# The next head pair's query and key work moved ahead of the present pair's output and retention end, on three engines

## What is computed

```python
def hybrid_layer(x, ...):
    proj = (_rms(x) * norm1_g) @ w_in
    aq, ak, av, rw, rq, rk, rv, rg, gates = _split(proj, IN_SIZES)
    aq = _rms(aq.reshape(B, T, ATTN_Q_HEADS, HEAD_DIM)) * attn_q_norm_g   # 8 heads of 64
    ak = _rms(ak.reshape(B, T, ATTN_KV_HEADS, HEAD_DIM)) * attn_k_norm_g
    o_a = sliding_window_attention(aq, ak, av, attn_sinks) @ w_attn_o
    o_b = rwkv7_time_mix(...) @ w_rwkv_o
    o_c = retention(rq, rk, rv, rg) @ w_ret_o
    ...

def retention(q, k, v, gate):
    qh, kh = _rotary(q, pos), _rotary(k, pos) * (d ** -0.5)
    s = jnp.einsum('bnihd,bnjhd->bnhij', qc, kc) * dmat
    inner = jnp.einsum('bnhij,bnjhe->bnihe', s, vc)
    kv = jnp.einsum('bnjhd,bnjhe,hj->nbhde', kc, vc, zeta)
    _, r_prev = lax.scan(step, 0, kv)            # R * chunk_decay + kv
    cross = jnp.einsum('bnihd,nbhde,hi->bnihe', qc, r_prev, xi)
    return _rms(inner + cross) * silu(gate)
```

## Time and profile before

| | |
|---|---|
| median of 3 runs | 3236.26 us (3235.94 to 3243.79) |
| the profiled execution | 3238.96 us |
| its span on the core | 3237.1 us |
| PE busy | 3112.4 us (96%) |
| DVE, ACT, POOL busy | 1140.9, 1100.4, 1432.6 us |
| mean granted clock of TensorE | 0.986 |

### The profile page before, as it was taken

The page is one execution under the profiler, slowest core; times in us unless marked ns, Lnnn a source line. Parts: engine busy times, 40 slices in busy tenths (PEclk is TensorE's granted clock), DMA queues, the critical chain, the costliest instruction groups (busy, mean ns, idle before and its releaser), DMA issues.

```text
span 3237.1 us, 52473 instructions
## 1 busy us (share of the span) xinstructions
PE 3112.4 (96%) x20754; PEld 2479.8 (77%) x20754; DVE 1140.9 (35%) x1645; ACT 1100.4 (34%) x1547; POOL 1432.6 (44%) x1824
## 2 busy tenths in 40 slices
PE   9999889999999999999989999999999998999999
PEld 6887678868878767887667888787788766788877
DVE  3026532361101446322555322226523255542210
ACT  4455543342222433113443322223311344432222
POOL 3532244635555444223325655565421242565555
PEclk9999999999999999999999999999999999999999
DMA  5233332213223232115214222233211331422223
GB/s 219 94 104 118 118 104 85 98 52 104 96 98 104 73 109 98 61 61 192 74 67 149 94 97 97 98 110 111 98 64 61 144 118 53 159 96 92 97 98 123
DMA packets 102130, 330.89 MB, mean 102 GB/s; under 512 B 10064, under 2 KB 10448, under 8 KB 101200
## 3 DMA queue, kind: packets, MB, share of 16 engines
q1 hardware_dynamic: 75088, 272.87, 24.7%
q10 hardware_dynamic: 26880, 55.65, 4.8%
HBM read 299.64 MB, written 28.84 MB: 101 GB/s over the span
## 4 chain that ended last, share of the span: by engine, by line
issue 41%; POOL 30%; PE 24%; DVE 2%; DMA 1%; ACT 1%; DVEq 0%; POOLq 0%; SPq 0%; ACTq 0%
POOL w_lo L317 30%; PE psum L346 19%; PE psum L682 4%; DMA H<-scratch 1%; DVEq L1507 0%; DMA arena<-in_w_ada 0%; POOLq L313 0%; PE psum L878 0%; PE psum L896 0%; PE psum L858 0%; POOLq L323 0%; PE psum L898 0%; DVE arena L2094 0%; DVE HL L1510 0%; DVE small L2079 0%
## 5 line engine op out<-in xcount | busy, mean ns | idle before, releaser
L317 POOL TENSOR_TENSOR w_lo<-w_raw,w_hi 128x256 fp32r<-128x256 f32 x1820 | 1432.4, 819 | 1800.2 <-ACT w_hi L932 1599.6
L346 PE MATMUL psum<-XH,w_hi 128*128 128x512 f32 x2592 | 1055.6, 407 | 9.5 <-DVE XL L1510 3.6
L346 PE MATMUL psum<-XH,w_lo 128*128 128x512 f32 x2592 | 1016.0, 392 | 0.0
L346 PE MATMUL psum<-XL,w_hi 128*128 128x512 f32 x2592 | 1014.7, 391 | 0.0
L932 ACT ACTIVATE w_hi<-w_raw 128x1024 fp32r<-128x1024 f32 x436 | 460.3, 1056 | 806.2 <-PE psum L346 690.2
L346 PEld LDWEIGHTS psum<-XH,w_hi 128*128 128x128 f32 x2592 | 490.0, 189 | 146.3 <-issue 28.3
L346 PEld LDWEIGHTS psum<-XL,w_hi 128*128 128x128 f32 x2592 | 489.5, 189 | 106.0
L346 PEld LDWEIGHTS psum<-XH,w_lo 128*128 128x128 f32 x2592 | 490.2, 189 | 102.9 <-issue 9.1
L346 PE MATMUL psum<-HH,w_hi 128*128 128x512 f32 x976 | 389.6, 399 | 26.4 <-DVE HL L1510 20.7
L346 PE MATMUL psum<-HL,w_hi 128*128 128x512 f32 x976 | 386.4, 396 | 0.0
L346 PE MATMUL psum<-HH,w_lo 128*128 128x512 f32 x976 | 384.5, 394 | 0.0
(11 more groups left out here) (328 smaller groups left out, 2389.4 us busy)
## 6 DMA issues: line engine op xcount, KB each, us to landing
w_raw<-in_fills SPq DMA_DIRECT2D x488, 512.0 KB, 3.2
scratch<-arena ACTq DMA_DIRECT2D x86, 256.0 KB, 2.0
arena<-scratch ACTq DMA_DIRECT2D x10, 1024.0 KB, 6.8
arena<-in_w_ada SPq DMA_DIRECT2D x4, 2048.0 KB, 19.4
H<-scratch ACTq DMA_DIRECT2D x4, 2048.0 KB, 15.0
scratch<-H SPq DMA_DIRECT2D x2, 2048.0 KB, 8.3
arena<-scratch ACTq DMA_DIRECT2D x2, 2048.0 KB, 9.3
arena<-scratch ACTq DMA_DIRECT2D x2, 1792.0 KB, 20.0
```

Of the source, the lines that this page charges most:

```text
L317: ins = nc.gpsimd.tensor_tensor(w_lo[:, to:to + FILL // 4], w_raw[:, of:of + FILL // 4], w_hi[:, to:to + FILL // 4].bitcast(F32), ALU.subt ...
L346: ins = mm(out_ap, wt[:, w:w + 128], xt[:, x0:x0 + T], start=first and k == 0 and o == 0, stop=last and k == n - 1 and o == 2)
```

## The change

On PE, `query_squares(p + 1)` and `rotate(p + 1)` are issued ahead of the attention output and the retention output of pair p, where they stood behind both. On ACT, `query_rstd(p + 1)` is issued ahead of the copy of the attention output and the square of the retention output. On DVE, `attend` is cut in three: `operands(p)`, the middle, and `retained(p)`; `operands(p + 1)` is issued between the state of pair p and its retention end. Three buffers change, since two pairs now overlap: the square of the retention output goes to `kz_t` (before `t1`), the retention end works in `rs` (before `t2`), and the last operation of the operands, which writes `qx`, waits for `rt_o` of the pair before. Nothing is added to or taken from the arithmetic.

```diff
@@ attend on PE
                     pe.wait_ge(sem("at_ptc"), 2 * n + 2)
+                    if p < PAIRS - 1:
+                        query_squares(p + 1)
+                        rotate(p + 1)
                     for b in range(NBLK):
...
                     ins.then_inc(sem("rt_o"), 1)
-                    if p < PAIRS - 1:
-                        query_squares(p + 1)
-                        rotate(p + 1)
                     fill(ATT[p][6])
                     pe.wait_ge(sem("rt_sq"), n + 1)
-                    mm(bank(2), C("blk1", 128), rt("t1", T), start=True, stop=True).then_inc(sem("rt_var"), 1)
+                    mm(bank(2), C("blk1", 128), rt("kz_t", T), start=True, stop=True).then_inc(sem("rt_var"), 1)
@@ attend on ACT
+                    if p < PAIRS - 1:
+                        query_rstd(p + 1)
                     act.wait_ge(sem("at_o"), n + 1)
                     fn(at("q", T, p * T), bank(4), ACT.Copy)
                     act.wait_ge(sem("rt_o"), n + 1)
-                    fn(rt("t1", T), bank(3), ACT.Square).then_inc(sem("rt_sq"), 1)
+                    fn(rt("kz_t", T), bank(3), ACT.Square).then_inc(sem("rt_sq"), 1)
                     takes(ATT[p][5])
-                    if p < PAIRS - 1:
-                        query_rstd(p + 1)
                     act.wait_ge(sem("rt_var"), n + 1)
@@ DVE
-                def attend(p):
+                def operands(p):
...
+                    if p:
+                        dve.wait_ge(sem("rt_o"), n)
                     tt(chunks(rt("qx", T), 128), chunks(rt("qr", T), 128), bc(TB("xi", 128, 128 * p), 4), ALU.mult).then_inc(sem("rt_qk"), 1)
+
+                def attend(p):
+
+                    n = l * PAIRS + p
                     dve.wait_ge(sem("at_sc"), n + 1)
...
                     ins.then_inc(sem("rt_r"), 1)
-                    dve.wait_ge(sem("rt_rs"), n + 1)
-                    tt(rt("t2", T), bank(3), rt("rs", T), ALU.mult)
                     drain()
-                    tt(q, rt("t2", T), A(RG, T, p * T), ALU.mult).then_inc(sem("rt_done"), 1)
-
+
+                def retained(p):
+
+                    dve.wait_ge(sem("rt_rs"), l * PAIRS + p + 1)
+                    tt(rt("rs", T), bank(3), rt("rs", T), ALU.mult)
+                    drain()
+                    tt(A(RQ, T, p * T), rt("rs", T), A(RG, T, p * T), ALU.mult).then_inc(sem("rt_done"), 1)
+
+                operands(0)
                 for p in range(PAIRS):
                     attend(p)
+                    if p < PAIRS - 1:
+                        operands(p + 1)
+                    retained(p)
```

## The result

| | before | changed |
|---|---|---|
| median (runs) | 3239.34 us (4; 3235.94 to 3243.79) | 3206.14 us (4; 3203.85 to 3211.54) |
| ratio | | 0.9899, 95% interval 0.9879 to 0.992 |
| span of the profiled execution | 3237.1 us | 3202.4 us |

The kernel is 1.0% faster: 33.2 us between the medians, where 32.3 us were forecast; the time itself is 3206.14 us, where 3204.0 was forecast. The median of the kernel before is 3.1 us higher here than in the table of the kernel before, which had one run fewer. Two later measurements of the same kernel, each on its own chip beside the kernel before, gave 0.9904 (0.9889 to 0.9919) and 0.9909 (0.9893 to 0.9926), 31.8 and 28.7 us.

The account below looks back on a forecast made before the run. PE bounds the kernel, held in attention by DVE's queue; steps between pairs' scores save 15.92 and 16.35 us, 32.3 in all, taking the median 3236.26 to 3204.0 us. Range with the first rival: 3197 to 3218 us.

Parts of the forecast that it names:

- What bounds the kernel, and the place: PE, busy 96% of the span; its longest sum of waits at line 858 for DVE, 18.2 us.
- The sum: Steps from one pair's scores to the next's: 15.92 us saved in layer 1, 16.35 in layer 2, 32.3 in all.
- PE's own move: 0: Squares and rotations 2.28 us, only moved; line 906's cover for ACT's square falls from 4.0 to 1.7 us; cost 0.
- The new wait for `rt_o`: 0: On DVE ahead of the last operand instruction, due about 1584.1; `rt_o` comes at 1582.3, so it holds nothing.
- The operands, 7.1 us: DVE's nine operand instructions for the next pair begin at 1577.65 and last 7.1 us, to 1584.8.
- Of this about 8.7 the half clock: TensorE's half clock in pairs 2 and 3: some 1.6 plus 2.7 us a layer, about 8.7 of the 32.3 us.
- the first rival: TensorE's clock does not come back in attention, so the 8.7 us are not had: 3212.7 us; chance 0.12.
- given back behind the attention: Rival: the stage behind attention turns the gain into waits for transfers and weights, about 3226 to 3236 us; chance 0.04.
- DVE as the bound: Rival: DVE's lateness at `at_sc` becomes PE's at 878, six times; 7.0 us a pair for slower, 3246; chance 0.03.
- The threshold: DVE's lateness at `at_sc` costs PE nothing at line 878 until it is 0.9 us.

Follow-up runs that it names:

- e1: Changed kernel with VectorE's order of before (retained(p) ahead of operands(p + 1)); 3236.3 us against 3236.47 us for the kernel before, ratio 0.9996.
- e2: Changed kernel with TensorE's and ScalarE's order of before, only VectorE's new; 3209.7 us, ratio 0.9915 to the kernel before.
- e7: Changed kernel with five unused VectorE operations of 512 columns behind the retention end of pairs 0 to 2; 3228.9 us against 3236.6 us for the kernel before.
- e9: Kernel before with six idle products on PE ahead of line 858 in pairs 1 to 3; ratio 0.9992 to the kernel before.
- e3: Changed kernel with only ScalarE's order of before, query_rstd(p + 1) late again; 3225.8 us, ratio 0.9965 to the kernel before.

## Why the prediction was right, and where it was not

*What bounds the kernel, and the place.* Right: e1 gives back all of the gain by one move on VectorE. Wrong only in the rank: 858 was the third of PE's waits, not the first.

*The sum.* 32.3 us forecast, 32.0 measured in the two stretches, 33.2 between the medians. Steps 30.88, 30.36 and 30.36 us forecast; 30.84, 30.24 and 30.71 measured. The forecast of pair 2 was 0.35 us too low, because its wait at 878 stayed at 1.16 us; I had carried pair 3's 0.75 over to it, and pair 2 is the one with the weight piece ahead of its exponentials. Pairs 1 and 3 came as forecast, at 0.75 and 0.74.

*PE's own move: 0.* Right; line 906 never waits. ACT's square is over 1.46 us before it, where 1.7 us of cover were forecast (its start and PE's line 906, one from each order of time):

```profile
1577.37 0.60 ACT L1460 ACTIVATE H<-psum 128x512 f32<-128x512 f32 x1 [2.56 <-PE psum L901]
```

```profile
1579.43 1.02 PE L906 MATMUL psum<-H,con 128*128 128x512 f32 x2
```

*The new wait for `rt_o`: 0.* Right; line 2073's row above, at 1577.56, shows no idle time before it.

*The operands, 7.1 us.* The term was 1 us too long. It was read in pair 1, where two operations had been slowed beside POOL; pair 2 of the same trace took 6.1 us (1624.06 to 1630.13), and so do all in the new place. DVE's second gap is longer for it, 3.66 us against the 2.4 forecast. It cost nothing in the sum, but e2 showed how much closer to free ACT's and PE's moves are than I thought. The Trainium skill's rule on the shared interface (GPSIMD Engine Reference, 1. Specifications) agrees with e7: operations with two SBUF inputs, put beside POOL's weight work, took 5.39 us for five against the 3.8 expected.

*Of this about 8.7 the half clock.* This is the step that failed, though the sum did not. As bookkeeping it is fair: PE's busy time in the stretches fell by 4.7 and 4.8 us. As a cause it is about twice too large. By e9 the falls at the scores cost 0.5 us in pair 2 (1.6 forecast) and 1.7 in pair 3 (2.7 forecast), 4.6 us in both layers; the rest of what I booked on the clock is time for which DVE would have held PE at full clock too. The sum came out because it was added up from whole steps, and the change takes both away at once, the falls and DVE's lateness behind them. How a step is split between them never entered it, and the price that the first rival puts on the clock alone was not put to the test. The Trainium skill's penalty (TensorE: Matmul & The Clock Gate, Terms: throttled time times one less the ratio) would have given 10.3 us. It fits the falls behind line 878, 1.6 us for 3.4 in e3, e7 and e9, and not those at the scores, 0.5 us for 3.4 in pair 2, 1.7 for 6.8 in pair 3 and 0.6 for 6.8 in pair 1 of e1.

*The rivals.* The clock did come back, at 1.00 in both stretches, in all three profiles of the changed kernel. Nothing was given back behind the attention that the profile shows beyond its usual spread. DVE as the bound: e7 shows that price; what I had left out of it is that each of its six long pauses also brought a fall of the clock. The threshold was about right: in pair 1 DVE came 4.7 us late (1593.89 for its start of the softmax, 6.54 us behind the scores' start, against 1.89 in the change) and PE waited 3.8 us more, so 0.9 us were free.

## What to carry to other kernels

When one engine waits in a queue's order for a late operand and the next round's work stands behind it, move that work ahead; here one engine's order was worth 31 of 32 us, and the two others' moves under 1. Price a slow clock, or any slow stretch, by the same round of the loop with and without it, in the same kernel, and check that nothing else differs: pair 2 of e3 in its two layers is such a case, while pairs 1 and 2 of the kernel before looked alike although only one had a fall, because the other had a delay of its own. If an experiment removes a slow stretch and the time stays, look for a new one before you call it free. For edits worth a few us, measure a stretch between two fixed events in the trace, which repeated here to 0.1 us at full clock where whole runs spread over some 8 (3203.85 to 3211.54).

## What the runs showed that I had not expected

A fall of TensorE's clock cost from a tenth to nearly half of its length, by where it fell: 0.6 us for 6.8 at line 858 in pair 1 of e1, 0.5 for 3.4 in pair 2, and 1.6 us for 3.4 behind line 878 in e3, e7 and e9.

And the pause ahead of a fall need not be long: it fell behind pauses of 2.21 us in e9 and e3, and in layer 1 of the changed kernel behind the 1.81 us at 1676.37, just past the end of the stretch:

```profile
1676.60:1680.10 3.50, 3.50 (x9) 2.74 (x9) 2.29 (x1) 1.82 (x3) 1.91 (x3) 0.51 0.99 362
```

The length of the pause does not decide it alone. In e3 the same pause of 2.21 us in the same pair was followed by a fall in layer 1 and by none in layer 2; the changed kernel's 1.81 us pause was followed by none in layer 2; and of the 3.04 us pauses in layer 1 of the kernel before, pair 1's had none behind it and pair 2's had one. Why stays open.
